# Transposed keys copied by two engines from four PSUM banks, bias and mask in one set of products, sample rows turned back early

## The reference, cut to what matters

```python
def sparse_attend(q, k_sel, v_sel, rel_b, valid):
    ...
    logits = jnp.einsum('bqkgd,bqskd->bqkgs', qg, k_sel).astype(jnp.float32) * (Dh ** -0.5)
    logits = logits + rel_b.astype(jnp.float32).reshape(B, Q, K, B_KV_HEADS, B_GQA).transpose(0, 1, 3, 4, 2)
    logits = jnp.where(valid[:, :, None, None, :], logits, -jnp.inf)
    p = jax.nn.softmax(logits, axis=-1).astype(v_sel.dtype)
    o = jnp.einsum('bqkgs,bqskd->bqkgd', p, v_sel)
...
def hier_moe(n, w_group, b_group, w_router, b_router, w_gate, w_up, w_down):
    ...
    for e in range(N_EXPERTS):
        h = jax.nn.silu(xf @ w_gate[e]) * (xf @ w_up[e])
        y = y + combine[:, e:e + 1] * (h @ w_down[e])
```

## Time and profile before

| | |
|---|---|
| runs | 1355.77, 1347.23, 1347.88 us |
| median | 1347.88 us |
| profiled execution | 1346.19 us, its span 1344.3 us |
| granted TensorE clock, mean | 0.964 |
| TensorE busy | 1245.4 us (93% of the span) |
| VectorE, ScalarE, GpSimd busy | 488.6, 199.0, 52.1 us |
| read from memory | 333.72 MB |

### The profile page before, as it was taken

One profiled execution on the slowest core, in us unless ns is written; L12 is line 12 of the kernel. 1 busy time (PEld: TensorE's weight loads), 2 busy tenths in 40 slices (PEclk: granted clock), 3 DMA queues, 4 the chain that ended last, 5 costly groups with the idle time before them and its releaser, 6 DMA issues.

```text
span 1344.3 us, 13342 instructions
## 1 busy us (share of the span) xinstructions
PE 1245.4 (93%) x5528; PEld 583.5 (43%) x5528; DVE 488.6 (36%) x993; ACT 199.0 (15%) x412; POOL 52.1 (4%) x68
## 2 busy tenths in 40 slices
PE   6999999999999888999998939999999999999995
PEld 4343443344444454777775633333333333333332
DVE  4000184299456320111124651333343333333333
ACT  2101223201222352000124220000000000000000
POOL 0020000000000012000000010000000000000000
PEclk8999999999999987999998969999999999999998
DMA  8755532454333456743465276999999999999972
GB/s 256 288 161 104 162 97 78 153 176 157 125 100 122 147 196 242 268 131 130 143 229 227 91 284 280 428 427 427 426 427 428 425 428 426 427 428 425 407 322 71
DMA packets 72600, 345.08 MB, mean 257 GB/s; under 512 B 13660, under 2 KB 17532, under 8 KB 55164
## 3 DMA queue, kind: packets, MB, share of 16 engines
q1 hardware_dynamic: 55952, 295.23, 55.9%
q0 software_dynamic: 8608, 41.95, 8.4%
q10 hardware_dynamic: 7980, 7.05, 2.3%
HBM read 333.72 MB, written 10.49 MB: 256 GB/s over the span
## 4 chain that ended last, share of the span: by engine, by line
PE 79%; DVE 11%; ACT 4%; DMA 3%; issue 2%; DVEq 0%; SPq 0%; ACTq 0%
PE PS L634 17%; PE PS L1176 16%; PE PS L922 14%; PE PS L1196 9%; PE PS L1140 5%; DVE X L2044 3%; PE PS L611 2%; DVE X L1729 2%; DVE top L1728 2%; DMA ring<-in_w_in 1%; PE PS L1185 1%; PE PS L869 1%; PE PS L1144 1%; PE PS L752 1%; DVE NC L2064 1%
## 5 line engine op out<-in xcount | busy, mean ns | idle before, releaser
L634 PE MATMUL PS<-ring,NC 128*128 128x512 f32 x704 | 320.0, 599 | 2.8 <-issue 1.6
L1176 PE MATMUL PS<-ring,NC 128*64 128x512 f32 x832 | 195.5, 604 | 1.4 <-DVE NC L2055 1.4
L634 PEld LDWEIGHTS PS<-ring,NC 128*128 128x128 f32 x704 | 128.5, 190 | 153.9 <-issue 150.7
L922 PE MATMUL PS<-NC,ring 128*128 128x288 f32 x768 | 190.5, 407 | 1.7 <-DVE X L1854 0.6
L922 PEld LDWEIGHTS PS<-NC,ring 128*128 128x128 f32 x768 | 144.3, 190 | 42.1 <-issue 2.9
L2041 DVE TENSOR_TENSOR X<-X,PS 128x1024 f32<-128x1024 f32 x68 | 83.0, 1221 | 150.5 <-PE PS L1140 141.2
L1176 PEld LDWEIGHTS PS<-ring,NC 128*64 128x64 f32 x832 | 54.5, 137 | 133.4 <-issue 131.6
L1196 PE MATMUL PS<-ring,NC 128*64 128x512 f32 x416 | 97.2, 622 | 6.1 <-ACT NC L1621 5.7
L1140 PE MATMUL PS<-XNN,NC 64*128 64x512 f32 x256 | 73.4, 654 | 5.7 <-DVE small L2090 5.2
L1619 ACT ACTIVATE NC<-PS,small 64x512 f32<-64x512 f32 x16 | 10.9, 681 | 443.0 <-PE PS L1176 443.0
L2069 DVE COPY XNN<-PS 128x1024 f32<-128x1024 f32 x16 | 19.6, 1225 | 123.9 <-PE PS L1196 123.9
(11 more groups left out here) (383 smaller groups left out, 1071.7 us busy)
## 6 DMA issues: line engine op xcount, KB each, us to landing
ring<-in_w_gate SPq DMA_DIRECT2D x26, 2048.0 KB, 16.5
ring<-in_w_up SPq DMA_DIRECT2D x26, 2048.0 KB, 19.1
ring<-in_w_down SPq DMA_DIRECT2D x26, 2048.0 KB, 17.9
ring<-in_w_in SPq DMA_DIRECT2D x36, 1024.0 KB, 5.1
ring<-in_w_out SPq DMA_DIRECT2D x16, 1024.0 KB, 5.1
XNN<-in_w_gate SPq DMA_DIRECT2D x8, 2048.0 KB, 16.2
NC<-in_w_up SPq DMA_DIRECT2D x8, 2048.0 KB, 19.5
XNN<-in_w_down SPq DMA_DIRECT2D x4, 2048.0 KB, 16.2
```

The lines of the kernel that those rows point to most:

```text
L634: last = mm(acc(n, t)[:, 0:width], lhs[:, kt, t * 128:(t + 1) * 128], slot(m)[:, k, 0:width], start=kt == 0, stop=kt == KT - 1)
L922: last = mm(PS[:, j, 0:NT], slot(m)[:, k, 128 * j:128 * j + 128], src[:, kt, :], start=kt == 0, stop=kt == width * 4 - 1)
L1176: last = mm(PS[64 * half:64 * half + 64, 2, :], XT[:, 4 * (kt // 4 % 2) + kt % 4, kt // 8, :], w, start=kt == 0, stop=kt == KT - 1)
```

## The change

The keys' groups rotate over four banks, 4 to 7 (`key_bank`). ScalarE copies the even groups and VectorE the odd ones, each with a semaphore of its own (`kt_free`, `kt_laid`). The mask is written below the bias, into partitions 32 to 63 of the same tile, and one set of products with 64 rows of the array adds both. ScalarE loads the table for Exp ahead of the key copies, takes the first half's exponential one sequence earlier, and the second half's behind the copies of the first half's probabilities.

`add_squares` leaves the last square apart in `sq_tmp`, and the sums over partitions take `sq_sum` and `sq_tmp` in two products each. The fills ahead of the routing stand before the projection. The sample rows are turned back right behind the prompt rows, ahead of the ranks. The two small exponentials stand behind the second and the sixth copy.

With the experts, the step with the sample rows stands behind `hidden_t`, ahead of the wait for ScalarE's copy, and VectorE adds it behind the hidden layer's product, ahead of the next rows.

The diff, cut to what the steps speak of:

```diff
@@ -77,7 +77,8 @@
-    put("pick", ((r == b * 4 + q) & (h >= 0)).astype(np.float32).reshape(32, 256))
+    pick = ((r == b * 4 + q) & (h >= 0)).astype(np.float32).reshape(32, 256)
+    put("pick", np.concatenate([np.tile(np.eye(32, dtype=np.float32), (1, 8)), pick]))
...
@@ -335,7 +336,7 @@
-        maskS = PB[0:R, 1, :]
+        maskS = biasSm[R:2 * R, :]
...
@@ -856,19 +857,26 @@
+
+            def key_bank(g):
+
+                if g >= 4:
+                    pe.wait_ge(S(("kt_free", "kt_laid")[g % 2]), (g - 4) // 2 + 1)
+                return PS[:, 4 + g % 4, :]
...
                 for b in four:
                     for c in range(2):
                         for half in range(2):
-                            bank = kgroup()
+                            bank = key_bank(4 * b + 2 * c + half)
                             for i in range(4):
                                 last = tr(bank[:, i * 128:i * 128 + 128], keys_raw(b)[:, 4 * half + i, c, :], ident)
                             last.then_inc(S("kt_ready"), 1)
-                pe.wait_ge(S("kt_free"), groups[0])
+                pe.wait_ge(S("kt_free"), 8 * (x + 1))
+                pe.wait_ge(S("kt_laid"), 8 * (x + 1))
                 for i, (a, z) in enumerate(KEYCUT):
...
@@ -878,12 +886,10 @@
                 last.then_inc(S("s_qk"), 1)
                 if x == 0:
                     pe.wait_ge(S("topkS"), 1)
-                for what in range(2):
-                    for i, (a, z) in enumerate(KEYCUT):
-                        for d in four:
-                            lhs = (cc("ident", R)[:, 0:R], cc("pick", R)[:, 32 * d:32 * d + 32])[what]
-                            last = mm(PS[32 * (d % 4):32 * (d % 4) + 32, 3 * x + i, 0:z - a], lhs,
-                                      (biasSm[0:R, a:z], maskS[:, a:z])[what], start=False, stop=what == 1)
+                for i, (a, z) in enumerate(KEYCUT):
+                    for d in four:
+                        last = mm(PS[32 * (d % 4):32 * (d % 4) + 32, 3 * x + i, 0:z - a], cc("pick", 64)[:, 32 * d:32 * d + 32],
+                                  biasSm[0:64, a:z], start=False, stop=True)
                 last.then_inc(S("s_logits"), 1)
...
@@ -973,10 +979,13 @@
                         g = 4 * q + h
                         mem_key_transposes(g // 2, g % 2)
                     if (q, h) == (1, 2):
-                        pe.wait_ge(S("h_squares"), 1)
+                        pe.wait_ge(S("h_squares"), 2)
                         for t in range(2):
-                            mm(PS[:, 5, t:t + 1], sq_sum[:, t * 128:t * 128 + 128], cc("ones")[:, 0:1], start=True, stop=True)
-                        mm(PS[:, 5, 2:2 + R], cc("ones"), sq_sum[:, T:NT], start=True, stop=True).then_inc(S("h_sums"), 1)
+                            for sq in (sq_sum, sq_tmp):
+                                mm(PS[:, 5, t:t + 1], sq[:, t * 128:t * 128 + 128], cc("ones")[:, 0:1],
+                                   start=sq is sq_sum, stop=sq is sq_tmp)
+                        mm(PS[:, 5, 2:2 + R], cc("ones"), sq_sum[:, T:NT], start=True, stop=False)
+                        mm(PS[:, 5, 2:2 + R], cc("ones"), sq_tmp[:, T:NT], start=False, stop=True).then_inc(S("h_sums"), 1)
...
             pe.nop().then_inc(S("moe_free"), 2)
-            pe.wait_ge(S("h_squares"), 2)
+            pe.wait_ge(S("h_squares"), 4)
             for t in range(3):
-                last = mm(PS[0:ROWS[t], 7, t:t + 1], sq_sum[:, t * 128:t * 128 + ROWS[t]], cc("ones")[:, 0:1],
-                          start=True, stop=True)
+                for sq in (sq_sum, sq_tmp):
+                    last = mm(PS[0:ROWS[t], 7, t:t + 1], sq[:, t * 128:t * 128 + ROWS[t]], cc("ones")[:, 0:1],
+                              start=sq is sq_sum, stop=sq is sq_tmp)
...
                     last.then_inc(S("row_turned"), 1)
-            turn_rows(0)
-            turn_rows(1)
+            for t in range(3):
+                turn_rows(t)
             pe.wait_ge(S("picked"), 1)
             for t in range(4):
                 rows = ROWS[t] if t < 3 else 128
@@ -1113,7 +1123,6 @@
                     last = mm(PS[0:rows, 5, 16 * t:16 * t + 16], lhs, AS[0:ROWS[u], u, :],
                               start=u == 0, stop=u == min(t, 2))
             last.then_inc(S("rank_ready"), 1)
-            turn_rows(2)
             pe.nop().then_inc(S("moe_free"), 2)
...
@@ -1208,11 +1217,13 @@
                     pe.wait_ge(S(f"moe_in{lot % NRING}"), 16 * (lot // NRING + 1))
                     return ring_at[lot % NRING]
                 pe.wait_ge(S("xt_laid"), e + 1)
-                gate_up(landed, lambda s: combine_step(e - 1, s) if e else None)
+                gate_up(landed, lambda s: combine_step(e - 1, s) if e and s < 4 else None)
                 pe.wait_ge(S(f"xg_in{(e + 1) % 2}"), 16 * ((e + 1) // 2 + 1))
                 rows_t((e + 1) % 2).then_inc(S("xt_ready"), 1)
                 pe.wait_ge(S("hidden"), e + 1)
                 hidden_t().then_inc(S("ht_ready"), 1)
+                if e:
+                    combine_step(e - 1, 4)
                 pe.wait_ge(S("ht_laid"), e + 1)
                 pe.wait_ge(S("y_out_psum"), e + 1)
                 down(landed).then_inc(S("moe_free"), 1)
...
+            act.preload_act_table(ACT.Exp)
             for b in range(8):
                 if b == 4:
                     act.wait_ge(S("s_qk"), 1)
                 for c in range(2):
-                    for half in range(2):
-                        g = 4 * b + 2 * c + half
-                        act.wait_ge(S("kt_ready"), g + 1)
-                        A(keys_t(b)[:, c, 512 * half:512 * half + 512], PS[:, 6 + g % 2, :], ACT.Copy).then_inc(S("kt_free"), 1)
-                if b == 5:
+                    g = 4 * b + 2 * c
+                    act.wait_ge(S("kt_ready"), g + 1)
+                    A(keys_t(b)[:, c, 0:512], PS[:, 4 + g % 4, :], ACT.Copy).then_inc(S("kt_free"), 1)
+                if b == 4:
                     act.wait_ge(S("s_max"), 1)
                     A(PB[:, 0, :], PSF[:, 0:NKEY], ACT.Exp, bias=st_neg[:, 0:1], accum_out=st_sum[:, 0:1])\
                         .then_inc(S("s_exp"), 1)
-            act.wait_ge(S("s_max"), 2)
-            A(PB[:, 1, :], PSF[:, 1536:1536 + NKEY], ACT.Exp, bias=st_neg[:, 1:2], accum_out=st_sum[:, 1:2])\
-                .then_inc(S("s_exp"), 1)
             g = 32
             for x in range(2):
+                if x:
+                    act.wait_ge(S("s_max"), 2)
+                    A(PB[:, 1, :], PSF[:, 1536:1536 + NKEY], ACT.Exp, bias=st_neg[:, 1:2], accum_out=st_sum[:, 1:2])\
+                        .then_inc(S("s_exp"), 1)
                 for part in range(3):
                     act.wait_ge(S("kt_ready"), g + 1)
...
-            route_exp(0)
-            for g in range(4):
+            for g in range(12):
                 rows_out(g)
-            route_exp(1)
-            for g in range(4, 12):
-                rows_out(g)
+                if g in (1, 5):
+                    route_exp(g // 4)
...
-            def sample_softmax(x):
+            def lay_keys(b):
+                if b == 4:
+                    dve.wait_ge(S("s_qk"), 1)
+                for c in range(2):
+                    g = 4 * b + 2 * c + 1
+                    dve.wait_ge(S("kt_ready"), g + 1)
+                    V.tensor_copy(keys_t(b)[:, c, 512:1024], PS[:, 4 + g % 4, :]).then_inc(S("kt_laid"), 1)
...
+            for b in range(4):
+                lay_keys(b)
+            sample_max(0)
+            lay_keys(4)
+            lay_keys(5)
+            sample_probs(0)
+            lay_keys(6)
+            lay_keys(7)
+            sample_max(1)
+            sample_probs(1)
...
+            def add_squares(h, k, stage):

                 if k == 0:
                     own(TT(sq_sum, h, h, ALU.mult))
-                else:
+                elif k < KT - 2:
                     own(TT(sq_tmp, h, h, ALU.mult))
                     own(TT(sq_sum, sq_sum, sq_tmp, ALU.add))
+                elif k == KT - 2:
+                    own(TT(sq_tmp, h, h, ALU.mult))
+                    TT(sq_sum, sq_sum, sq_tmp, ALU.add).then_inc(S("h_squares"), 1)
+                else:
+                    dve.wait_ge(S("h_squares"), 2 * stage + 1)
+                    TT(sq_tmp, h, h, ALU.mult).then_inc(S("h_squares"), 1)
...
+                add_squares(hT1[:, k, :], k, 0)
+            own(V.memset(MQZ, 0.0))
...
                     mem_sample_norm()
+            own(V.memset(xss, 1.0))
+            own(V.memset(route, 0.0))
             for k in range(KT):
                 if k % 4 < 3:
...
             for e in range(NEXP):
                 if e:
-                    combined(e - 1)
+                    combined(e - 1, range(4))
                 slot_weights(e % 2, tabF[:, e:e + 1], tabF[:, NBLK + e:NBLK + e + 1])
                 dve.wait_ge(S("silu"), e + 1)
```

(28 more changed lines are left out.)

3 lines of the change are left out of this document (removed).

## The result

| | runs | median us | range |
|---|---|---|---|
| before | 4 | 1349.2 | 1347.2 to 1355.8 |
| changed | 4 | 1330.5 | 1328.3 to 1332.8 |

The ratio is 0.987, with a 95% interval of 0.984 to 0.989: 1.3% faster, where 1.7% was forecast. The profiled execution took 1329.5 us, its span is 1327.6 (before: 1346.2 and 1344.3), 16.7 less in place of 21.9.

The account below looks back on a forecast made before the run. TensorE was taken to bound the kernel (79% of the chain), with the DMA engines also full in the experts. Terms -14.3 + 0.6 - 0.3 - 7.9 = -21.9 from 1346.19 us; forecast 1325.5 us, range 1316 to 1336.

Parts of the forecast that it names:

- First half's keys: Sample attention, first half's key transposes and copies: cold start, then TensorE sets the pace; key products 2.7 us earlier.
- Bias and mask: Sample attention, first half: one set of products of 1.84 us in place of two of 3.67, -1.8 us.
- Second half's keys: Sample attention, second half's key transposes and copies: 8.8 us in place of 15.2, -6.4 us.
- Logits and softmax: Sample attention, second half's logits to the first value product: 7.5 us in place of 12.2, -4.7 us.
- Value products: End of sample attention: first half 2.2 us shorter, but +3.5 us for a gather wait and half a cold start.
- Norms: Sums over partitions at two norms: +0.6 us at the first, -0.3 us at the second.
- Routing: Turning the sample rows back ahead of the ranks: 0 us, or +0.5 if an exponential came late.
- Experts: Expert loop: 0.95 us less per expert until the weights set a period of 30.7 us; -7.9 us in all.
- the weights don't bind: Rival: the experts gain the whole 14.3 us, with no cap by weight loads; 1319.6 us, chance 0.12.
- the experts gain nothing: Rival: the moved step costs as much in its new place, or the stream has no reserve; 1333.9 us, chance 0.13.
- The half gain of the sample attention: Rival: the clock stays at 1.2 GHz in the sample attention, which gains 8 us; 1332.3 us, chance 0.15.
- The slower case: Rival: TensorE's waits for lots lower the clock in the last eight experts; about 1368 us, chance 0.04.

Follow-up runs that it names:

- scalar_only: The changed kernel with four banks for the transposed keys, but ScalarE alone copying, 16 copies in each half: 1331.6 us.
- probs_early: The changed kernel with the first half's probabilities turned ahead of and behind the second half's key products: 1332.0 us.
- light_after: The changed kernel, loading only half the bytes of each of the down projection's two lots for experts 1 to 15: 1317.7 us.
- experts_only: The kernel before with the experts' part of the change alone, the sample rows' step behind the hidden transposes: 1341.6 us.
- sample_only: The kernel before with the sample attention's part of the change alone: 1338.5 us.
- light_before: The kernel before, loading only half of each lot of the down projection for experts 1 to 15: 1350.5 us.
- the two filled kernels: The kernel before with four products, or three transposes, without use behind each expert's hidden transposes: 1352.4 and 1344.2 us.
- warm_keys: The changed kernel with sample 4's values gathered early and 36 products without use in two waits ahead of the sample attention: 1329.4 us.

## Why the prediction was right, and where not

1. *First half's keys:* -2.7 forecast, measured 9.82 us to the key products in place of 12.69, -2.9. Cold at the start, as argued.
2. *Bias and mask:* -1.8; 1.89 us for one set (492.15 to 494.04) in place of 3.67 for two. So 64 rows cost as good as nothing over 32 (1.84).
3. *Second half's keys:* 8.8 us forecast, 8.83 measured. The sum of the steps held, and TensorE's clock was 1.00 from 485 to 510 us.
4. *Logits and softmax:* 7.5 us forecast, 9.06 measured (502.87 to 511.93). Products and bias took the 5.5; turning and copying the probabilities took 3.5 in place of 2.0, because ScalarE's first copy began 1.3 us after the first transpose (0.7 in the second half), and its second waited too. In `scalar_only` it took 2.0. `probs_early` shows that it mattered little: there the first value products came 0.9 us earlier, and the second half's no earlier than elsewhere.
5. *Value products:* this is the term that was mis-sized. I had the wait for gathers (2.4 us) and half a cold start (1.1). In four of the five profiles with four banks and the gathers in the old order the first half runs at 2.4 GHz; there the wait is 3.4 to 4.2 us and the second half's products take 6.7 to 7.1, a full cold start of 2.5 to 2.9. In the fifth, that of the changed kernel, the clock fell earlier, and from the first value product to the output projection it took 14.9 us, near my 15.2, by luck. So the stage gains 10 to 11 us in four profiles and 13.5 in this one; I had 14.3. (My six terms put the output projection at 521.2; I wrote 520.9.) The gathers that I let land at 512.0 to 514.4 landed at 516.3 on the axis of the profile before (521.11 less the 4.8 of the start). Their rate was as assumed: on that axis their first packet moves at 493.1 and 97% of the packets are through at 513.9, some 390 GB/s. What I had left out is the tail, 2.4 us until the last packets of the last gather are in and its semaphore is seen. A transfer of 1152 KB (`L545`, issued right behind) already runs beside this tail; no run here moves it away.
6. *Norms:* +0.6 and -0.3 forecast. The first cost 0.7 (its sums start 8.8 us earlier than before, the next product 8.1), but 0.8 came back before the second, where a stretch of products lay more at 2.4 GHz (4.90 us in place of 5.67); that is not the change's doing. The second gained 1.0: twelve records took 1.27 us, about as long as six before, since the clock was at 2.4 GHz and not at 1.2, and the idle of 1.04 us went whole:

```profile
758.36 1.27 PE L1098 MATMUL PS<-cst,XNN 128*128 128x1 f32 x12
```

7. *Routing:* 0, and so it was: the offset between the traces is 10.0 us behind the sums and 10.1 at the first gate.
8. *Experts:* -7.9 forecast, -6.6 measured. Per expert 0.90 us in place of 0.95: `gate_up` gives 1.15 and VectorE's earlier product 0.20, but `down` comes 1.94 us after `hidden_t` begins in place of 1.50, 0.44 more where I had 0.24, since the hidden transposes occupy 0.95 us (874.83 to 875.78) and not 0.75. The mechanism was right: period 29.2 first, the first wait for a lot at the start of the tenth expert, then 30.5 to 30.8.

```profile
1061.12 0.61 PE L1185 MATMUL PS<-XNN,NC 128*64 128x512 f32 x1 [2.06 <-DMA NC<-in_w_up]
```

What TensorE would gain without a cap was 17 to 18.6 and not 14.3, but the cap swallowed the difference: the weights' stream, whose pace I took from bytes and GB/s, sets the end by itself. The extra block began at 1274.35, 7.3 us earlier on the axis of before (7.9 forecast), and took 0.7 longer than before.

Summed up by the four profiles, 10 to 11 us for the sample attention, 0.5 for norms and routing (without the 0.8 that the clock gave) and 6.6 for the experts are 17 to 18; the medians differ by 18.8. I had 21.9. What is missing is the 3 to 4 us of step 5 and the 1.3 of step 8; the rest is within the spread of the runs.

Of the rivals, "the weights don't bind" is refuted by `light_after`, "the experts gain nothing" by `experts_only`. The half gain of the sample attention did not come, but the shortfall lay in that direction. The slower case needed cold stretches at each wait for a lot. The windows show the clock at 1.00 through waits of up to 2.1 us there. The Trainium skill (TensorE: Matmul & The Clock Gate, HAM oscillation) tells of a kernel whose TensorE goes cold at every wait for DMA, with waits of about 3 to 5 us. The trace agrees at the value products, with waits of 3.4 to 4.2 us. The waits for lots, of 1.1 to 2.1 us, are shorter than those of that kernel, so they neither bear the rule out nor speak against it.

## What to carry to other kernels

When transfers already fill the DMA engines beside a busy TensorE, work out bytes per period over GB/s before making TensorE faster: the gain is capped by that quotient, and the reserve of loaded tiles says only from when on. Where a stage ends in a wait for a transfer, look at which transfer could start while the DMA engines stand still, and expect the clock to make the wait dearer than its length (here 2.5 to 2.9 us more behind waits of 3.4 to 4.2). For copies out of PSUM the number of banks came first (two in place of four cost 5.5 us), the second copier hardly counted (1.1 us, within the noise). And a single profile can mislead: the changed kernel's shows its stage 3 us shorter than the four others with the same order do.

## What the runs showed of the hardware

- Two waits of 0.35 and 0.47 us, 1.0 us apart, were followed in 3 of 16 experts by a stretch at 1.2 GHz that cost 1.7 us, at the same experts in `sample_only` and `light_before`. With the second wait filled there was none. Single waits of 1.1 to 2.1 us for lots were followed by none either. In the sample attention the length of a wait alone did not decide: of eight waits of 0.9 to 1.7 us, one in each of eight kernels with the new order, ahead of the first half's value products, three (1.27, 1.31, 1.52) were followed by products that ran in part at 1.2 GHz (5.9 us in place of 4.2) and five (0.92, 1.31, 1.33, 1.40, 1.67) were not. Those of 2.3 us and more ahead of the second half's all were.
- A float32 product of 128x128 stands in the trace as two records, 0.23 to 0.29 us in all; a transpose as one, 0.18 in the fill and 0.12 in a long row of them.
- A copy of 128x512 from PSUM takes 0.69 us on VectorE (L1846) and 0.60 on ScalarE; in a row VectorE needs 1.29 for two, ScalarE 4.10 for eight, so 0.60 and 0.51 each.
- Open: behind the second half's bias set VectorE's maximum started 0.4 to 0.9 us later than behind the first half's, in the changed kernel and six others (ScalarE's first copy as well in most), but not in `scalar_only` and `warm_keys`. It is not the change's: with the old sample attention it shows in `before`, `light_before` and `experts_only` (0.3 to 0.9) and not in the two filled kernels. No run here tells why.
